# A gate matrix built by adding transfers, and expert tables streamed in pairs of blocks

## The reference

```
q = (xb @ w_pq).reshape(-1, PEER_HEADS, 2, PEER_DK_HALF)
sc = jnp.einsum('thpd,hpkd->thpk', q, sub_keys)
v1, i1 = lax.top_k(sc[:, :, 0], 16)
v2, i2 = lax.top_k(sc[:, :, 1], 16)
...                                  # the 16 best pairs (i1, i2) of each head
gate = jax.nn.softmax(top_sc, axis=-1)
hid = jax.nn.gelu(jnp.einsum('td,thkd->thk', xb, u_tab[eidx]))
return jnp.einsum('thk,thkd->td', gate * hid, v_tab[eidx])
```

## Time and profile before

| | us |
|---|---|
| runs | 1771.45, 1772.53, 1777.73 |
| median | 1772.53 |
| profiled run, its own time | 1774.21 |
| span of its instructions | 1771.7 |

### The profile page before, as it was taken

The page is one execution under the profiler, slowest core; times in us unless marked ns, Lnnn a source line. Parts: engine busy times, 40 slices in busy tenths (PEclk is TensorE's granted clock), DMA queues, the critical chain, the costliest instruction groups (busy, mean ns, idle before and its releaser), DMA issues. The chain is left out here.

```text
span 1771.7 us, 19797 instructions
## 1 busy us (share of the span) xinstructions
PE 1660.0 (94%) x6994; PEld 1229.4 (69%) x6994; DVE 1209.8 (68%) x2606; ACT 365.1 (21%) x906; POOL 695.7 (39%) x601
## 2 busy tenths in 40 slices
PE   7998999999778998799889999999999999999987
PEld 6887888877665786687776666666666666566633
DVE  2252112697899778899987998677666666656676
ACT  1041123125321244634750001101000000000101
POOL 0000000132324438622765655545544546544542
PEclk9998999999889999899999999999999999999999
DMA  5532543675757959997999999999999999999997
GB/s 190 184 101 95 167 142 119 230 256 191 249 191 271 389 167 351 350 322 231 367 336 409 406 409 409 409 406 410 404 409 409 406 410 407 387 409 410 409 379 279
DMA packets 224337, 552.61 MB, mean 312 GB/s; under 512 B 15696, under 2 KB 112080, under 8 KB 223600
## 3 DMA queue, kind: packets, MB, share of 16 engines
q0 software_dynamic: 82944, 302.03, 44.4%
q1 hardware_dynamic: 118304, 237.69, 36.7%
q10 hardware_dynamic: 22992, 11.64, 2.2%
HBM read 534.22 MB, written 16.42 MB: 311 GB/s over the span
## 5 line engine op out<-in xcount | busy, mean ns | idle before, releaser
L786 POOL DMA_INDIRECT M<-in_u_tab,IDX x288 | 334.6, 1162 | 709.0 <-DVE PEER L1731 341.1
L793 POOL DMA_INDIRECT M<-in_v_tab,IDX x288 | 357.0, 1240 | 342.0 <-DVE X L1752 264.3
L1076 PE MATMUL PSB<-XN,M 128*128 128x256 f32 x2048 | 463.6, 380 | 8.0 <-ACT M L1298 4.5
L1084 PE MATMUL PSB<-M,HST 128*128 128x512 f32 x1024 | 460.7, 595 | 7.0 <-DMA M<-in_v_tab 3.4
L1076 PEld LDWEIGHTS PSB<-XN,M 128*128 128x128 f32 x2048 | 389.0, 191 | 107.4 <-issue 52.6
L1731 DVE CUSTOM_DVE_ANT_0 M<-M,XN 128x1024 f32<-128x1024 f32 x288 | 351.3, 1221 | 125.2 <-DMA M<-in_u_tab,IDX 117.8
L1752 DVE SCALAR_TENSOR_TENSOR X<-M,PEER,X 128x1024 f32<-128x1024 f32 x256 | 328.0, 1281 | 98.3 <-DMA M<-in_v_tab,IDX 84.5
L835 PE MATMUL PSB<-M 128*128 128x256 f32 (+1 forms) x1536 | 366.5, 400 | 6.8 <-DVE M L1386 6.1
L835 PEld LDWEIGHTS PSB<-M 128*128 128x128 f32 x1536 | 297.0, 195 | 67.8 <-DVE M L1386 7.0
L1084 PEld LDWEIGHTS PSB<-M,HST 128*128 128x128 f32 x1024 | 194.4, 191 | 210.5 <-issue 195.4
L842 PE MATMUL PSB<-M 128*128 128x256 f32 (+1 forms) x928 | 211.4, 387 | 1.1 <-ACT M L1262 0.7
(11 more groups left out here) (213 smaller groups left out, 1085.4 us busy)
## 6 DMA issues: line engine op xcount, KB each, us to landing
M<-in_u_blocks SPq DMA_DIRECT2D x128, 512.0 KB
M<-in_v_tab SPq DMA_DIRECT2D x128, 512.0 KB
M<-in_w_in SPq DMA_DIRECT2D x24, 1024.0 KB
M<-in_w_pq SPq DMA_DIRECT2D x16, 1024.0 KB
gate_spill<-M ACTq DMA_DIRECT2D x11, 1024.0 KB, 17.7
M<-gate_spill SPq DMA_DIRECT2D x16, 704.0 KB
M<-in_w_out SPq DMA_DIRECT2D x8, 1024.0 KB
M<-in_w_mq SPq DMA_DIRECT2D x8, 1024.0 KB
```

Source lines behind the costliest of these rows:

```text
L786: pool.indirect_dma_start(out=UA[:, s % RR, :], out_offset=None, in_=utab, in_offset=bass.IndirectOffsetOnAxis(ap=IDX[:, n:n + 1], axis=0) ...
L793: pool.indirect_dma_start(out=VA[:, s % RR, :], out_offset=None, in_=vtab, in_offset=bass.IndirectOffsetOnAxis(ap=IDX[:, n:n + 1], axis=0) ...
L1076: last = pe.matmul(PSB[:, 4 + b % 2, 0:2 * P], UBLK[:, b % SR, c, :], XN[:, 1:3, c * P:(c + 1) * P], start=(c == 0), stop=(c == DC - 1))
L1084: last = pe.matmul(PSB[:, 2 * t + hf, :], WR[:, b % WRING, t * P:(t + 1) * P], VBLK[:, b % SR, hf * 512:(hf + 1) * 512], start=(b == 0), s ...
```

## The change

Tile 1's gate matrix is no longer multiplied. SP first writes zeros over its eight chunks in DRAM (16 stores of 512 KB ahead of eight weight blocks, from a zero tile that VectorE clears). Its routing (`routed_by_pairs`) computes for each of 128 (head, k) columns the place in `gate_spill` of every token's expert, and softmax is done by pairs of heads. Then GpSimd issues 128 indirect DMAs that add one gate for each of 128 tokens to DRAM, two behind each of the slots 28 to 91 (counted from 0), with a wait for all earlier ones before every 16th. The first gate group is read when all of them are done. The 32 `oh` and `gb` of tile 1, its `tt`, its staging and its eight spills are gone; in tile 2 three chunks are spilled as before.

The tables are laid out by the host as 64 pairs of blocks with 8 KB in a row for each partition, and are loaded by 1 MB transfers into rings of two pairs. The second v pair lies where the one-hot tiles were, and is loaded after the last `gb`. The scores of tiles 2 and 4 take the place of those of tiles 0 and 1, so ScalarE waits for their routing.

In the plan d and v lie later in the dense part, 16 and not 5 `lk` stand ahead of `tt`, and no `lk` between the last `gb` and w(0).

```
-SR = 3
+SCATTERS = NK
+SCATTER_SLOT = 28
+SCATTERS_A_SLOT = 2
+SCATTER_US = 1.0
+SR = 2
+PAIRS = NBLK // 2
...
-G0_SLOTS = 29
+G0_SLOTS = 26
+AHEAD_RT = 14
+AHEAD_OH = 6
+LATE_TURNS = 3
...
-            t_dve += dve_us(x)
+            t_dve += dve_us(x) + SCATTER_US * (x[0] == "d" and SCATTER_SLOT <= x[1] * TOPK + x[2] < SCATTER_SLOT + SCATTERS // SCATTERS_A_SLOT)
...
-    out += merged(late, extra) + merged(rt(2, 3), ahead[:3])
+    out += merged(merged(late + rt(2, 3), extra), ahead[:AHEAD_RT])
...
+                if NW < i <= NW + 8:
+                    for k in range(2 * (i - NW - 1), 2 * (i - NW)):
+                        sp.dma_start(spill[k, :, 0:FIRST_STAGED, :], ZERO.rearrange("p (c x) -> p c x", c=FIRST_STAGED)).then_inc(zeroed, 16)
...
+            def u_pair(k):
+                if k >= SR:
+                    sp.wait_ge(lk_done, 2 * (k - SR + 1))
+                sp.dma_start(UPAIR[k % SR], ublocks[k]).then_inc(ublk_in[k % SR], 16)
...
-                if seg == ("lk", HRING - 8):
+                if seg == ("w", 0):
                     sp.wait_ge(relaid_s, 64)
                     sp.wait_ge(oh_used, len(SMALL))
+                    v_pair(1)
...
+                    sp.wait_ge(scattered, 16 * SCATTERS)
                     for k in range(GRING):
                         gate_group(k)
...
+            def scatter(n):
+
+                if n == 0:
+                    pool.wait_ge(zeroed, 16 * NBLK // GRP)
+                if n % (2 * TOPK) == 0:
+                    pool.wait_ge(gates_done, softs_before(DENSE[0], n // (2 * TOPK)) + 1)
+                if n and n % TOPK == 0:
+                    pool.wait_ge(scattered, 16 * n)
+                pool.indirect_dma_start(out=gates, out_offset=bass.IndirectOffsetOnAxis(ap=SIDX[:, n:n + 1], axis=0),
+                                        in_=GATE[:, DENSE[0], :, :].rearrange("p h k -> p (h k)")[:, n:n + 1], in_offset=None,
+                                        compute_op=ALU.add).then_inc(scattered, 16)
...
+                    if i * TOPK + s >= SCATTER_SLOT:
+                        for _ in range(min(SCATTERS_A_SLOT, SCATTERS - nscatter)):
+                            scatter(nscatter)
+                            nscatter += 1
...
             def const():
+                dve.memset(ZERO, 0.0).then_inc(zero_set, 1)
+                dve.wait_ge(const_ok, 2)
...
```

More of the change, by code:

```diff
@@ L165, in rt, with soft, routed_by_pairs @@
     return [("rt", t, pair, k) for k in range(7)]
-def soft(t):
-    return [("sme", t), ("smd", t)]
+def soft(t, part=0):
+    return [("sme", t, part), ("smd", t, part)]
+def routed_by_pairs(t):
+    s, held = [], []
+    for pair in range(PH // 2):
+        pieces = rt(t, pair)
+        s += pieces[:2] + held + pieces[2:] + soft(t, pair)[:1]
+        held = soft(t, pair)[1:]
+    return s + held
 def merged(a, b):
@@ L212, in plan @@
     first = [x for pair in range(PH // 2) for x in rt(0, pair)] + soft(0)
-    second = [x for pair in range(PH // 2) for x in rt(1, pair)] + soft(1)
+    second = routed_by_pairs(1)
     extra = first[:7] + merged(first[7:], slots[:one]) + merged(second, slots[one:early])
-    extra += [("tt", 1)] + merged(batches(1), slots[early:mid])
+    extra += slots[early:mid]
     late_slots, slots = slots[mid:last], slots[last:]
     t_pe = t_dve = 0.0
-    gone, held, late, odd = set(out), [], [], 0
+    gone, late, odd = set(out), [], 0
     for w in work:
[L221 to L224, removed]
         while (extra or late) and w[0] in LONG and t_dve < t_pe:
             odd += 1
-            if late and (odd % 2 or not extra):
+            if late and (odd % LATE_TURNS or not extra):
                 out.append(late.pop(0))
@@ L327, in jobs_of @@
         return [(seg, "A")]
-    if k == "gb" and seg not in SMALL:
-        return [(seg, "A")]
-    if k in ("dt", "o", "mo") or seg == ("tt", 1):
+    if k in ("dt", "o", "mo"):
         return [(seg, "D")]
@@ L359 @@
 ROUTED = {s[1:3]: n for n, s in enumerate(x for x in PLAN if x[0] == "rt" and x[3] == 6)}
-SOFTS = [s[1] for s in PLAN if s[0] == "sme"]
+SOFTS = [s[1:] for s in PLAN if s[0] == "sme"]
 def routed_up_to(t):
@@ L1713, in route, with soft_sum @@
                 pieces[(t, pair)][k]()
-            def soft_sum(t):
-                gate = GATES[:, :, :] if t == NP else GATE[:, t, :, :]
-                n, heads = softs_before(t), 2 if t == NP else PH
+            def soft_sum(t, part):
+                gate, _ = soft_heads(t, part)
+                n, heads = softs_before(t, part), gate.shape[1]
                 dve.wait_ge(exps_done, n + 1)
```

248 lines of the change are left out of this document (114 added, 134 removed).

## The result

The changed kernel takes 1843.13 us in the median of four runs (1839.46 to 1854.77), the kernel before 1771.45 to 1777.73 beside it. The ratio is 1.0409, 95% interval [1.0379, 1.044]: **4.1% slower**. The prediction (1761, range 1742 to 1804) was wrong, in sign and in range. The profiled execution took 1839.46, its span 1837.7.

What follows compares the result with a forecast made beforehand. TensorE barely holds the last stage from 938 us; VectorE runs without a gap for a hundred us before it. Terms -25 + 7.5 + 5 + 1 = -11.5 on the 1771.7 us span: about 1761, range 1742 to 1804.

Steps and rivals of the forecast that it cites:

- What bounds the kernel, and the last stage: From 938 us TensorE barely holds the last stage, 6.89 us a block; six more gathers there cost 5 us.
- Gate products go: Before the first table product: 28.7 us of TensorE's products and 7.6 of waits for ScalarE go, start at 780.6 us.
- The junction, 134 us of VectorE's work: First table product to w(0): VectorE works 134 us without idling, not 108.7; second product of block 0 comes 25 us earlier.
- GpSimd, the step that failed: First table product to slot 92: 19 slots at 5.5 us plus 10, 114.5 against VectorE's 107, costing 7.5 us.
- 6.0, 7.0, 8.2: Prices in us for a GpSimd slot of four transfers: gather means, short and long by turns, four of 1.75.
- 44 slots have 300 us: enough on average: Dense part, before the first table product: GpSimd's slots there fit, tight where 12 stand in 50 us; no cost counted.
- The break-even: Nothing is won once a GpSimd slot after the first table product costs 6.1 us; 0.5% slower from 6.6.
- GpSimd binds: slower: Rival, 31%: GpSimd's slots after the first table product set the time; 1788 at 6.9 us a slot, 1812 at 8.2.
- a scatter dearer than any gather: The case beyond the range's upper end of 1804 us, a slot of 7.8 us; some 15%.
- Traffic of the elements: The scatters' 16,384 elements take 29 us of the 16 DMA engines' time, even with the eight spills that go.
- Zeroing, start and pairs: Zero stores hidden, start 1 us later; 1 MB pairs gain nothing by the rows, 8 us at most, left out.
- The Trainium skill: VectorE two-input instructions and GpSimd SBUF reads exclude each other, so scatters beside d or v pay long; 1 MiB transfers rate best.

Runs made afterwards that it cites:

- e1: The changed kernel with its 128 scatters left out and all else kept: 1756.74 us, 0.9921 of the kernel before.
- e7: The changed kernel with only the first 64 scatters, two behind each of slots 28 to 59, all in the dense part: 1786.29 us.
- e5: The changed kernel with half of the scatters (heads 0 to 3), one behind each of the 64 slots: 1771.12 us, 1.0003 of the kernel before.
- e11: The kernel before with only the tables' layout and loads changed to pairs of blocks in 1 MB transfers: 1771.34 us, 1.0012 of the kernel before.
- e14: The changed kernel once more, unchanged, as the measure for runs beside it: 1847.34 us, 1.0452 of the kernel before.
- e15: The changed kernel with each scatter replaced by four chained memsets of 440 columns on GpSimd, no transfer: 1825.51 us, 1.0309 of the kernel before.

## Why the prediction was wrong, point by point

- **What bounds the kernel, and the last stage**: right. 6.89 us a block, 838.1 us against 838.5 predicted. The match of the stage may be partly luck: with pairs alone it is 828 to 830, so the rest of the change adds 8 to 10 us there and not 5.
- **Gate products go**: 36.3 us won at the first table product was the forecast; without scatters it is 52.4 (e1). The step counted what goes from TensorE and left out TensorE's waits for VectorE, which are 11 us shorter in e1; the prediction had put VectorE's 32 comparisons at nothing there. With the scatters 23.5 were left.
- **The junction, 134 us of VectorE's work**: 153 in e1. The step took VectorE to have no gap and missed 17.6 us behind ScalarE's gelus. The two errors cancel: e1's span is 1754.3, the sum without GpSimd's term gives 1752.7.
- **GpSimd, the step that failed.** The term was +7.5 us; the scatters cost 86 (e1). It had three numbers. *The price*: 5.5 us for a slot of four; measured 7.41 in the mean from slot 44 on. A scatter was taken at a gather's price and takes 1.62 us undisturbed and 1.78 in the mean; its bounds, though, "6.0, 7.0, 8.2", had it inside. *The count*: 19 slots, with the dense part at nothing because "44 slots have 300 us: enough on average". That is 6.8 us a slot, enough at 5.5 and not at the two upper bounds: at 7.41 they need 326 us. e7 shows 30 us for the 32 slots there, and for that lateness 22 slots' scatters, not 19, were left at the first table product (44 from 794 us on). *The slope* that follows: 19 us for each us of slot, measured 55. By the prediction's own formula a slot of 7.41 gives 1797; the other 46 us lie in the slope: the slots counted at nothing, and the 16 to 20 us of the 86 that holding GpSimd alone doesn't give.
- **The break-even** of 6.1 us a slot was near: e5 stands at 6.18 and draws level with before. The same number is before's own pace (6.07 from slot 44 on, slots 44 and 92 at 575.7 and 866.8 us). So the sum had the sign right for any price above it, and took the wrong price; what the pace adds is that above it every slot of the stretch counts, not only the last 19.
- **The rival "GpSimd binds: slower"** is what happened, for 31%, "a scatter dearer than any gather" being its part outside the range. Of its two reasons the adding carried it: 0.61 of the 0.68 us by which an undisturbed scatter is longer than a gather. The one against, that the short duration comes back when VectorE has gaps, holds in part: scatters with no VectorE instruction of over 1 us beside them took 1.62 us (44 of them), the others 1.87 (84), but half of these, too, took no more than 1.63.
- **Traffic of the elements**: forecast 29 us of the engines' time for all 128 scatters, measured 36 for 119 by the estimate above; that it is hidden is right for the most part (the hold without transfers gives 67 to 69 of the 86 us).
- **Zeroing, start and pairs**: right as far as can be told; nothing to be seen in e1 and e11.
- **The Trainium skill**: the prediction set "SBUF — State Buffer", section "Who interferes with whom", against the rows. Gathers of the kernel before took 0.945 us with no VectorE instruction of over 1 us beside them (130) and 1.28 with one (446), but 57% of the latter were under 1 us, as short as the others. The trace agrees in direction; that the exclusion lasts for the whole of every such instruction, or that every scatter beside a d or v pays for it, it doesn't show. The rule of the Trainium skill on 1 MiB a transfer ("DMA: Bandwidth & Descriptors", section "Rules for kernel authors") made no difference here (e11, 1.0012): blocks of half of that were fast enough for TensorE.

## What to carry to other kernels

Before moving work to an engine that feeds another one row by row, compare its price for one step with the pace at which the steps are used, over the whole stretch: below it the work is cheap but not free (14 us for 64 scatters at one a slot, 30 at two), above it every step counts. Take an operation that no row shows at the upper end of its bounds wherever that comparison turns on it. And when a piece is moved in an in-order queue, look at what it makes wait there: a late row, a softmax or a gate group behind loads each took back what the move was to win.

## What the hardware showed that I had not expected

- An indirect DMA that adds one 4-byte element for each of 128 partitions holds GpSimd for 1.62 us undisturbed, one that writes them 1.00, one that gathers 128 rows of 4 KB 0.94, each with 0.30 behind it. So 512 B cost GpSimd more than 512 KB: its price doesn't go by bytes.
- The adding one puts 144 packets in the queue, the writing one 32 for the same elements; an added element took 38 ns of a DMA engine (an estimate, from e14 and e15).
- While TensorE waited at the junction its granted clock was 0.78 to 0.82 in the mean of the window, against 1.00 in the last stage: a mean of stretches at 1.2 and at 2.4 GHz. It was back at 1.00 when the tables streamed.
